# Another order for the delta-rule rounds of a two-layer decoder step

## The chip, the cores and the metric

The kernel runs on one core of a Trainium2 chip. The metric is device time in microseconds (us) of one execution, median of several; lower is better. A core has TensorE (PE, with its weight loads as PEld), VectorE (DVE), ScalarE (ACT), GpSimd (POOL) and SyncE (SP), which in this kernel issues nearly all DMAs. Each engine works off its own list of instructions in order and waits on semaphores for the others.

## The reference, cut to what matters

One inference step of a two-layer trunk, on 512 prompt tokens and 8 x 4 sample tokens: a retention layer, then a gated delta-rule layer, each followed by a mixture of experts. All is float32. The change touches only the delta-rule mixer:

```python
def _gated_delta_chunked(q, k, v, g, beta, s0):
    def step(s, xs):
        ...
        a = jnp.where(strict, jnp.einsum('bhid,bhjd->bhij', kb, ki) * decay, 0.0)
        sol = lax.linalg.triangular_solve(eye + a, rhs, left_side=True, lower=True, unit_diagonal=True)
        u = sol[..., :DN_DV] - sol[..., DN_DV:] @ s
        att = jnp.einsum('bhid,bhjd->bhij', qi, ki) * decay
        o = (qi * jnp.exp(G)[..., None]) @ s + att @ u
        s = (s * jnp.exp(g_last)[..., None]
             + jnp.einsum('bhjd,bhjv->bhdv', ki * jnp.exp(g_last - G)[..., None], u))
        return s, o

def _deltanet_mixer(h, s0, buf, w_in, ...):
    p = h @ w_in
    qkv, buf_new = _causal_conv(p[..., :DN_CONV_CH], buf, conv_w)   # 4 taps, 4096 channels
    qkv = jax.nn.silu(qkv).astype(F32)
    ...
    o, s = _gated_delta_chunked(q, k, v, g, beta, s0.astype(F32))
    o = _rms_norm(o, norm_g) * jax.nn.silu(z...)
    return o.reshape(B, L, DN_VW).astype(h.dtype) @ w_out, ...
```

There are 16 value heads. The prompt has a state that starts at zero; each of the 8 sample sequences brings its own states and gets them back updated.

## The kernel before

The function `delta` (from L1010) computes this mixer. The 16 heads go in four **groups** of four heads; the 512 prompt tokens go in four **chunks** of 128. Chunk `i` of group `g` has the number `x = 4 g + i`, and two chunks share one run `p` of the triangular solve.

The input product is cut into 78 **units** (the list `UNITS`), each of eight matmuls (the items `("mm", U, k)`, k from 0 to 7). Units of features have 512 columns in the first ten and 272 columns afterwards (two halves for one 128-channel column); units of the gate z have 512 columns; a unit of sample rows issues 64 small matmuls, all at k = 7. Units 10 + 21 g to 30 + 21 g belong to the time in which group g is worked on and bring the features of the next group.

One list, the generator `schedule`, sets the order on all engines at once. Each engine walks through it and does its part of every item, in that order. The steps of a group are:

- **A1, AD, A3, A5** (each chunk): transposed keys, decays, scalars, attention and solve matrices.
- **L0, X, P, X5, P5, X6, P6** (each run of the solve): levels of a block inversion. PE multiplies, DVE masks, subtracts and transposes; for P5, X6 and P6 ACT makes copies (L1830, L1838, L1841) on which the next PE step waits.
- **CV, C1, C2, C3, C4, C5** (each chunk, one after another because of the state S): transposed values; products with S; u; the update of S and the output `ob` (DVE L2116, L2127; ACT squares the output, L1818); the norm (DVE L2132, POOL power L1974); in C5 DVE multiplies `ob` by the norm and z (L2140), PE transposes it (L1494), ACT copies it to `oTr` (L1823), SP stores it.
- **SA, SB, SX, SP, S1, S2, S3, SO, SN, SE** (samples of the group). S1 multiplies the sample states with keys and queries (L1596), for head pair 0, then 1; S2 solves. **S3** comes four times a group, for each head pair and each half of the sequences: DVE spreads u over four sequences (`ue`, L2236), PE multiplies (L1617), DVE updates eight states (L2242). After the second half SP stores the states of the pair (L1300) and, when they are out, loads the next pair's into the same tile (L1238).
- **CO** writes rows of the convolution out.

`merge` puts lists together by a place between 0 and 1 for each entry. In groups 0 to 2 the mm items are spread over the first 95% of the group's steps, so that the last C3, C4 and C5 of a group stand without any. In group 3 there are few units left, and eight products of the modulation (AM, four parts each, L221) and four tiles of the first part of the output product (OP, eight matmuls each, L1660) are spread instead.

Around the mm items hang the convolution and its activation. At k = 3 of unit U, DVE convolves unit U-1 if that completes a column: one `tensor_scalar` and three `scalar_tensor_tensor` (L2052, L2054), in one go. At k = 7 ACT applies silu to it (L1777). SP loads the next blocks of weights (2 MB each, L177) at k = 0 of the first unit of a block, through a ring of three slots.

## Time and profile before

| | |
|---|---|
| median of 3 runs | 2101.22 us (2099.69 to 2122.41) |
| profiled execution | 2105.92 us, of which the span of instructions is 2104.1 us |
| mean granted TensorE clock | 0.929 |
| busy: PE, DVE, ACT, POOL | 1820.2, 794.4, 379.0, 357.6 us |
| delta rounds, groups 0 to 3 | from about 1038 to 1747 us of the span |

The profile shows one execution. A row of the timeline gives the start, the duration, engine, line, operation, what is written and read, how many instructions are merged, and in brackets how long the engine stood idle before it and who released it. The clock of PE is given as a share of full speed; 0.5 is the lower of its two levels.

### The profile page before, as it was taken

The numbers are of one execution on the slowest core, as the hardware profiler recorded it, in microseconds if no ns is written. First come the engines' busy times: TensorE is split into PE (matmuls) and PEld (weight loads), VectorE is DVE, ScalarE is ACT, GpSimd is POOL, SyncE is SP. The second block draws the span as 40 slices with busy tenths as digits, with TensorE's granted clock in tenths as the row PEclk, the third lists the DMA queues.
The fourth block names the chain that finished last, engine by engine and source line by source line (L and its number), as shares of the span: only waits on it lengthen the run. The fifth ranks groups of instructions, "written<-read, shape, count | busy, mean of one in ns | idle before, by whom it ended". The sixth has DMA issues, their size and how long they took to land. (4 is left out here: it accounts for less than half of the span.)

```text
span 2104.1 us, 37009 instructions
## 1 busy us (share of the span) xinstructions
PE 1820.2 (87%) x15669; PEld 970.9 (46%) x15669; DVE 794.4 (38%) x1655; ACT 379.0 (18%) x839; POOL 357.6 (17%) x461
## 2 busy tenths in 40 slices
PE   6999999999999678957979989988989888949990
PEld 4344444444434333324556665765665463433320
DVE  0233332323424320034665455546544442450006
ACT  1001000000000011124332242232223110002112
POOL 0020110201103100022421022031113000320006
PEclk9999999999999879987999999999999999969995
DMA  9546657465551299988431034033124548158993
GB/s 327 190 164 232 257 200 256 143 230 200 171 201 50 86 390 401 399 302 266 135 97 48 12 114 126 9 112 92 43 59 170 195 158 270 60 215 320 401 359 137
DMA packets 237630, 399.62 MB, mean 190 GB/s; under 512 B 17993, under 2 KB 94017, under 8 KB 237410
## 3 DMA queue, kind: packets, MB, share of 16 engines
q1 hardware_dynamic: 231514, 375.75, 51.3%
q0 software_dynamic: 5952, 21.50, 2.7%
q8 instruction: 125, 2.05, 0.4%
q14 instruction: 39, 0.32, 0.0%
HBM read 303.71 MB, written 93.51 MB: 189 GB/s over the span
## 5 line engine op out<-in xcount | busy, mean ns | idle before, releaser
L686 PE MATMUL bank<-ring,hT 128*128 128x512 f32 x704 | 319.5, 601 | 1.9 <-DVE ret_qk L904 1.9
L1361 PE MATMUL bank<-hT,ring 128*128 128x272 f32 x768 | 217.0, 417 | 0.0
L686 PEld LDWEIGHTS bank<-ring,hT 128*128 128x128 f32 x704 | 129.6, 191 | 170.0 <-issue 169.8
L2541 PE MATMUL bank<-expert_w,exp_xT 128*32 128x512 f32 x1152 | 178.1, 626 | 15.3 <-DMA expert_w<-in_moe_w_gu_dram 11.4
L1361 PEld LDWEIGHTS bank<-hT,ring 128*128 128x128 f32 x768 | 140.7, 197 | 33.6 <-issue 8.9
L1355 PE MATMUL bank<-ring,hT 128*128 128x512 f32 x256 | 124.8, 616 | 0.0
L3354 PE MATMUL bank<-ring,oT 128*128 128x512 f32 x248 | 114.3, 622 | 0.8 <-PEq L580 0.8
L2541 PEld LDWEIGHTS bank<-expert_w,exp_xT 128*32 128x32 f32 x1152 | 47.9, 115 | 126.4 <-issue 121.2
L2637 DVE TENSOR_TENSOR exp_a<-bank,exp_sg 128x256 f32<-128x256 f32 x24 | 10.2, 424 | 218.9 <-ACT exp_sg L2619 218.9
L978 DVE SCALAR_TENSOR_TENSOR ret_Ss<-ret_Ss,ret_sdec,bank 128x512 f32<-128x512 f32 x64 | 45.0, 744 | 121.3 <-PE bank L772 121.3
L2054 DVE SCALAR_TENSOR_TENSOR dn_y<-dn_pre,dn_conv,dn_y 128x568 f32<-128x568 f32 x96 | 89.1, 928 | 3.4
L2565 PE MATMUL bank<-expert_w,exp_aT 128*32 128x512 f32 x576 | 87.2, 595 | 1.7 <-ACT exp_aT L2601 1.4
L3354 PEld LDWEIGHTS bank<-ring,oT 128*128 128x128 f32 x248 | 49.0, 199 | 62.0 <-issue 62.0
L1355 PEld LDWEIGHTS bank<-ring,hT 128*128 128x128 f32 x256 | 45.9, 194 | 44.6 <-issue 43.6
L1358 PE MATMUL bank<-hT,ring 128*128 128x512 f32 x128 | 57.8, 602 | 1.4 <-ACT dn_smpT L1764 1.4
L2541 PE MATMUL bank<-oT,exp_xT 128*32 128x512 f32 x384 | 56.5, 594 | 0.0
L493 ACT ACTIVATE hT<-bank 128x512 f32<-128x512 f32 (+1 forms) x26 | 13.4, 569 | 213.9 <-PE bank L483 213.9
L2593 DVE COPY exp_y<-bank 128x512 f32<-128x512 f32 x24 | 16.6, 691 | 89.3 <-PE bank L2565 89.3
L848 POOL TENSOR_TENSOR ret_gate<-ret_gate,ret_gn 128x512 f32<-128x512 f32 x16 | 20.3, 1269 | 176.1 <-ACT ret_gate L814 176.1
L3354 PE MATMUL bank<-end_extra,oT 128*128 128x512 f32 x112 | 49.2, 592 | 0.0
L221 PE MATMUL bank<-ring,cT 128*32 128x128 f32 x1280 | 49.1, 298 | 0.0
L1974 POOL TENSOR_TENSOR dn_rso<-dn_sso,eps 128x4 f32<-128x4 f32 x16 | 16.8, 1047 | 173.9 <-DVE dn_sso L2134 173.9
(531 smaller groups left out, 2719.3 us busy)
## 6 DMA issues: line engine op xcount, KB each, us to landing
expert_w<-in_moe_w_gu_dram SPq DMA_DIRECT2D x24, 2048.0 KB, 16.9
ring<-in_w_ada_dram SPq DMA_DIRECT2D x20, 2048.0 KB, 9.5
expert_outputs<-ret_zeros SPq DMA_DIRECT2D x15, 2048.0 KB, 10.4
expert_w<-in_moe_w_down_dram SPq DMA_DIRECT2D x24, 1024.0 KB, 17.4
ret_Ss<-in_state_ret_dram SPq DMA_DIRECT2D x32, 512.0 KB, 5.2
out_dram<-ret_Ss SPq DMA_DIRECT2D x32, 512.0 KB, 3.3
oT<-in_moe_w_gu_dram SPq DMA_DIRECT2D x8, 2048.0 KB, 20.6
ring<-in_dn_w_in_dram SPq DMA_DIRECT2D x8, 2048.0 KB, 9.2
```

Of the source, the lines that this page charges most:

```text
L221: last = pe.matmul(bank[NS * j:NS * (j + 1), 0:P], self.cT[:, k, :], self.ring[:, self.slot[w], k, P * j:P * (j + 1)], start=(k == 0), sto ...
L686: last = pe.matmul(ps[u % 2][:, :], core.hT[:, k, tok(t)], core.ring[:, core.slot[w], k, :], start=(k == 0), stop=(k == KD - 1))
L848: pool.tensor_tensor(gate[:, t, :], gate[:, t, :], gn[:, :], ALU.mult).then_inc(s["gate_done"], 1)
L978: dve.scalar_tensor_tensor(Ss[:, y % SLOTS, a, :], Ss[:, y % SLOTS, a, :], sdec[:, 1, h:h + 1], ps[2 + a][:, :], ALU.mult, ALU.add).then_i ...
L1355: mm = pe.matmul(ps[U % 2][:, :], core.hT[:, k, tok(c)], core.ring[:, core.slot[w], k, :], start=(k == 0), stop=(k == KD - 1))
L1358: mm = pe.matmul(ps[U % 2][:, :], core.ring[:, core.slot[w], k, c * P:(c + 1) * P], core.hT[:, k, 0:SEQ], start=(k == 0), stop=(k == KD - 1))
L1361: mm = pe.matmul(ps[U % 2][:, 0:HALF], core.ring[:, core.slot[w], k, c * P:(c + 1) * P], core.hT[:, k, half * HALF:(half + 1) * HALF], sta ...
L1974: pool.tensor_tensor(rso[:], sso[:], core.eps[:, 3:4].broadcast_to([P, 4]), ALU.pow).then_inc(s["rso_done"], 1)
L2054: ins = dve.scalar_tensor_tensor(y[:, 0:n], pre[:, F % 2, k:k + n], t.conv[:, ch, k:k + 1], y[:, 0:n], ALU.mult, ALU.add)
L2541: last = pe.matmul(ps[v][G * j:G * (j + 1), :], xT[:, v, k, G * j:G * (j + 1)], wgu[of[j] % SLOTS][:, k, :], start=(k == 0), stop=(k == KD ...
L2565: last = pe.matmul(ps[2 + c][G * j:G * (j + 1), :], aT[:, w % 2, k, G * j:G * (j + 1)], wdn[of[j] % SLOTS][:, k, c * W:(c + 1) * W], start ...
L3354: last = pe.matmul(ps[2 * (t % 2) + c][0:rows(t), :], values(t)[:, k, :], blocks[2 * (k // KD) + c][:, k % KD, :], start=(k == (KD if apar ...
```

## The change

Only the order of the steps of the delta rounds changes, and how they are cut; each instruction and its operands stay.

1. In groups 0 to 2 the first two units of the next group are taken out of the next group's spread. Their first twelve mm items stand ahead of the group's last C5, the other four behind it. In group 3 the last six OP items stand ahead of the last C5.
2. C5 is cut: its DVE part becomes the step OG, where C5 stood; the rest (PE transposes, ACT copy, SP store) is C5, now behind the next chunk's C3.
3. S3 is cut into UE (DVE spreads u), S3 (PE) and SU (DVE updates the states, SP stores and loads), with places of their own.
4. The solve steps get places written out by hand (SOLVE).
5. A convolution is done in two halves: taps 0 and 1 at k = 3, taps 2 and 3 at k = 5.
6. SP waits for the first `op_in` transfer before it issues the second.

```diff
-                out += [("CV", x + i), ("C1", x + i), ("C4", x + i - 1), ("C2", x + i), ("C5", x + i - 1), ("C3", x + i)]
-            return out + [("C4", x + NC - 1), ("C5", x + NC - 1)]
+                out += [("CV", x + i), ("C1", x + i), ("C4", x + i - 1), ("C2", x + i), ("OG", x + i - 1), ("C3", x + i),
+                        ("C5", x + i - 1)]
+            return out + [("C4", x + NC - 1), ("OG", x + NC - 1), ("C5", x + NC - 1)]
 
         def s_state(g, hp):
-            return [("S1", g, hp), ("S2", g, hp), ("S3", g, (hp, 0)), ("S3", g, (hp, 1))]
+            return [("S1", g, hp), ("S2", g, hp)] + [(what, g, (hp, half)) for half in range(2) for what in ("UE", "S3", "SU")]
...
-                         at={2: (0.05, 0.12, 0.2), 3: (0.55, 0.65, 0.72, 0.8, 0.86, 0.92, 0.98)})
+                         at={0: SOLVE, 2: (0.04, 0.09, 0.13, 0.18, 0.181, 0.23, 0.28),
+                             3: (0.55, 0.62, 0.67, 0.71, 0.76, 0.761, 0.81, 0.86, 0.89, 0.94, 0.99)})
             c = c_steps(g)
-            return out + merge(b_steps(2 * g + 1), c[:10]) + c[10:]
+            return out + merge(b_steps(2 * g + 1), c[:11], at={0: SOLVE}) + c[11:]
+        SOLVE = (0.02, 0.11, 0.18, 0.25, 0.31, 0.38, 0.44, 0.51, 0.57, 0.69, 0.79, 0.87, 0.95)
...
+            yield from products(first[1], first[1] + ahead)
+            for g in range(1, G):
+                mm, *body = list(products(first[g] + ahead, first[g + 1])), *group(g - 1)
+                yield from merge(body[:-1], mm, at={1: [SPREAD * (i + 0.5) / len(mm) for i in range(len(mm))]})
+                fill = list(products(first[g + 1], first[g + 1] + ahead))
+                yield from fill[:-4]
+                yield body[-1]
+                yield from fill[-4:]
+            even = lambda a, b, n: [a + (b - a) * (i + 0.5) / n for i in range(n)]
+            mm, body = list(products(first[G] + ahead, first[G + 1])), group(G - 1)
+            end = 1 - 1 / len(body)
+            yield from merge(body, mm, LAST, OUT, at={1: even(0, 0.2, len(mm)), 2: even(0.25, 0.94, len(LAST)),
+                                                      3: even(0.21, 0.5, 2 * KD) + even(0.5, 0.96, KD + 2) + [end] * (KD - 2)})
...
+                            sp.wait_ge(s["op_in"], 16)
                             sp.dma_start(core.hT[:, :, 2 * P:SEQ], oTd[:, 0:KD, 2 * P:SEQ]).then_inc(s["op_in"], 16)
...
-                    if what == "S3" and h[1] == 1:
+                    if what == "SU" and h[1] == 1:
                         n = 2 * x + h[0]
                         sp.wait_ge(s["sss_done"], 4 * (n + 1))
...
-                    if what == "C5":
+                    if what == "OG":
                         dve.wait_ge(s["rso_done"], x + 1)
...
+                    if what == "SU":
+                        hp, half = l
+                        n = 2 * g + hp
                         dve.wait_ge(s["s3_ps"], 2 * n + half + 1)
...
-                follow(lambda U: None, step, convolve)
+                follow(lambda U: None, step, lambda U: convolve(U, (0, 1)), LATE, lambda U: convolve(U, (2, 3)))
```

## Rows read from the trace of the kernel before

**Rows 1.** Windows, one for each group: PE, PEld, DVE, ACT, POOL busy, then clock.

```profile
1038.00:1221.00 183.00, 158.61 (x2002) 112.50 (x2001) 98.47 (x229) 52.20 (x135) 35.71 (x55) 0.94 0.20 59
1221.00:1395.00 174.00, 156.28 (x2006) 109.53 (x2006) 96.29 (x225) 54.04 (x133) 32.47 (x51) 0.95 0.25 77
1395.00:1571.00 176.00, 156.84 (x1998) 110.49 (x1997) 96.92 (x225) 50.53 (x129) 33.16 (x51) 0.95 0.27 81
1571.00:1747.00 176.00, 151.27 (x2329) 90.58 (x2327) 73.80 (x202) 42.98 (x89) 25.77 (x33) 0.91 0.54 178
```

**Rows 2.** Waits of PE over the four groups: total us, times, longest.

```profile
PE bank L1494 <- DVE dn_ob L2140: 34.7, 11, 6.7
PE bank L1617 <- DVE dn_ue L2236: 19.4, 10, 3.9
```

**Rows 3.** Windows at two points where PE's clock is low.

```profile
1170.00:1180.00 10.00, 8.29 (x57) 6.35 (x56) 5.55 (x12) 1.34 (x3) 0.33 (x2) 0.58 0.10 27
1390.00:1400.00 10.00, 5.76 (x43) 4.16 (x44) 3.55 (x5) 1.24 (x3) 4.43 (x6) 0.51 0.30 85
```

**Rows 4.** Timeline around the end of group 1.

```profile
1382.90 1.14 DVE L2140 SCALAR_TENSOR_TENSOR dn_ob<-dn_ob,dn_rso,dn_z 128x128 f32<-128x128 f32 x4 [1.12 <-POOL dn_rso L1974]
...
1386.64 1.12 DVE L2116 SCALAR_TENSOR_TENSOR dn_S<-dn_S,dn_egl,bank 128x128 f32<-128x128 f32 x4 [2.60 <-PE bank L1483]
...
1391.00 2.52 POOL L1981 TENSOR_TENSOR dn_km<-dn_qr,masks 128x512 f32<-128x512 f32 x2
1391.06 3.13 DVE L2140 SCALAR_TENSOR_TENSOR dn_ob<-dn_ob,dn_rso,dn_z 128x128 f32<-128x128 f32 x4 [1.12 <-POOL dn_rso L1974]
...
1394.24 1.12 PE L1494 MATMUL bank<-ident,dn_ob 128*128 128x128 f32 x4 [6.75 <-DVE dn_ob L2140]
```

**Rows 5.** Timeline: unbroken runs of input products, and a unit of sample rows.

```profile
1226.09 4.29 PE L1361 MATMUL bank<-hT,ring 128*128 128x272 f32 x18
...
1379.92 3.60 PE L1355 MATMUL bank<-ring,hT 128*128 128x512 f32 x8
...
1093.91 1.95 PE L1349 MATMUL bank<-ring,hT 128*32 128x128 f32 x64
```

**Rows 6.** Timeline around the first C5 of group 0.

```profile
1167.01 1.76 DVE L2177 TENSOR_TENSOR dn_TTf<-dn_TT,bank 32x256 f32<-32x256 f32 x4 [3.18 <-PE bank L1518]
1168.89 0.69 PE L1525 MATMUL bank<-dn_TTf,dn_A 32*32 32x32 f32 x32 [1.26 <-DVEq L2180]
...
1170.32 0.87 DVE L2187 COPY dn_X<-bank 32x256 f32<-32x256 f32 x2
...
1172.41 1.11 PE L1494 MATMUL bank<-ident,dn_ob 128*128 128x128 f32 x4 [1.72 <-DVE dn_ob L2140]
1172.82 2.50 DVE L2054 SCALAR_TENSOR_TENSOR dn_y<-dn_pre,dn_conv,dn_y 128x568 f32<-128x568 f32 x3
```

**Rows 7.** Timeline of group 0: the first S3 and the second S1.

```profile
1077.37 1.13 PE L1617 MATMUL bank<-dn_ue,dn_kds 32*128 32x512 f32 x4 [2.97 <-DVE dn_ue L2236]
...
1078.55 2.16 DVE L2242 SCALAR_TENSOR_TENSOR dn_SS<-dn_SS,dn_egls,bank 128x128 f32<-128x128 f32 x8 [1.23 <-PE bank L1617]
...
1099.94 3.62 PE L1596 MATMUL bank<-dn_SS,dn_km 128*32 128x128 f32 x64 [4.08 <-issue]
```

**Rows 8.** Timeline of group 1: sample states out and in, weights, and S1.

```profile
1265.13 1.02 SPq L1300 DMA_DIRECT2D out_dram<-dn_SS  x2
1268.45 2.43 SPq L1238 DMA_DIRECT2D dn_SS<-in_state_dn_dram  x2
1275.73 0.37 SPq L177 DMA_DIRECT2D ring<-in_dn_w_in_dram  x1
...
1275.97 1.95 PE L1596 MATMUL bank<-dn_SS,dn_km 128*32 128x128 f32 x64 [0.27 <-issue]
...
ring<-in_dn_w_in_dram SPq DMA_DIRECT2D x1, 2048.0 KB, 9.3
```

**Rows 9.** Timeline: the end of group 3.

```profile
1742.23 1.12 PE L1494 MATMUL bank<-ident,dn_ob 128*128 128x128 f32 x4 [3.90 <-DVE dn_ob L2140]
```

More of the change, by code:

```diff
@@ L1137, in schedule, with products @@
         def schedule():
-            first = [0] + [10 + 21 * g for g in range(G)] + [len(UNITS)]
-            for g in range(G + 1):
-                mm = []
-                for U in range(first[g], first[g + 1]):
+            first, ahead = [0] + [10 + 21 * g for g in range(G)] + [len(UNITS)], 2
+            def products(start, stop):
+                for U in range(start, stop):
                     for k in range(KD):
-                        mm.append(("mm", U, k))
+                        yield "mm", U, k
@@ L1145, in schedule @@
                         if k == 3 and U and samples(U - 1):
-                            mm.append(("ST", *unit(U - 1)[0:2]))
-                if g == 0:
-                    for item in mm:
-                        yield item
-                        yield from GATE.get(item[1:], ()) if item[0] == "mm" else ()
-                elif g < G:
-                    head = 2 * KD if g == 1 else 0
-                    yield from mm[:head]
-                    mm = mm[head:]
-                    yield from merge(group(g - 1), mm, at={1: [SPREAD * (i + 0.5) / len(mm) for i in range(len(mm))]})
-                else:
-                    even = lambda a, b, n: [a + (b - a) * (i + 0.5) / n for i in range(n)]
-                    yield from merge(group(g - 1), mm, LAST, OUT, at={1: even(0, 0.29, len(mm)), 2: even(0.3, 0.96, len(LAST)),
-                                                                      3: even(0.29, 0.5, 2 * KD) + even(0.5, 0.99, 2 * KD)})
+                            yield "ST", *unit(U - 1)[0:2]
@@ new lines, in schedule @@
+            for item in products(0, first[1]):
+                yield item
+                yield from GATE.get(item[1:], ()) if item[0] == "mm" else ()
+            yield from products(first[1], first[1] + ahead)
[6 more added lines that the diff above has]
+                yield from fill[-4:]
@@ L1200, in delta, with follow @@
         quad = lambda q: slice(NS * q, NS * (q + 1))
-        def follow(project, step, later=None, late=LATE):
+        def follow(project, step, later=None, late=LATE, rest=None):
             for item in schedule():
@@ L1209, in follow @@
                         later(item[1] - 1)
+                    if rest and item[2] == late + 2 and item[1] > 0:
+                        rest(item[1] - 1)
                 else:
@@ L2057, in convolve @@
                             chain(ins)
-                    ins.then_inc(s["conv_done"], 1)
+                        else:
+                            ins.then_inc(s["conv_done"], 1)
                 def chunk_step(what, x):
@@ L2227, in sample_step @@
                                                  ).then_inc(s["rs_done"], 1)
-                    if what == "S3":
+                    if what == "UE":
                         hp, half = l
```

15 lines of the change are left out of this document (9 added, 6 removed).

## The prediction

> **What bounds the kernel now.** I looked first for the stretch that the change touches: by its lines the delta rounds run from 1038 to 1747 us. The windows by group say that PE is busy 623 of these 709 us, DVE 365, ACT 200 [rows 1]. So PE is the bound, and what can be won is what it loses: 24 us of idle time in group 0, 18 in group 1, 19 in group 2, 25 in group 3, together 86. The clock column adds a second loss: a mean of 0.94, 0.95, 0.95 and 0.91 means that 11, 9, 9 and 16 us, together some 45, went missing as clock, part of it while PE stood idle anyway. The clock falls where PE has just been idle: 0.51 in the 10 us in which the wait of 6.75 us ends, 0.58 in those behind 1.26 and 1.72 us [rows 3, 4, 6]. 0.5 is 1.2 GHz, 1.0 is 2.4.
>
> The waits of PE name two steps for 54 of the 86 us: the transposes of C5, which wait for DVE's multiplication by norm and z (34.7 us, 11 times), and the product of S3, which waits for DVE's `ue` (19.4 us, 10 times) [rows 2]. The timeline then says why. At the end of a group there is no filler: after the last C3 come DVE's update of S, the output, the square, the reduction, POOL's power and DVE's multiplication, and PE stands for 6.75 us [rows 4]. In the middle of a group DVE works in order, with the convolution and eight state updates ahead of what PE waits for [rows 6, 7]. The rounds are followed by a stage that needs all of them, so time saved here shortens the kernel.
>
> **Part 1: two units around the last transposes.** In unbroken runs a product of 272 columns takes 4.29/18 = 0.24 us, one of 512 columns 3.60/8 = 0.45, a unit of sample rows 1.95 [rows 5]. Twelve of the first kind are 2.9 us. At the end of groups 0 and 1 the wait of 6.7 falls by that, and by some 0.4 for the four transposes of chunk 2, which now also stand there: 3.3 us each. At the end of group 2 the twelve items are the sample unit and four products of 512 columns, 1.95 + 1.8, with the transposes 4.1 us. At the end of group 3 six OP products (2.7) and the transposes take 3.1 of 3.90 [rows 9]. Sum: **13.8 us**. The products leave the next group's spread, which has work enough: 21 units either way. The remaining wait is the chain itself; its last link takes 3.13 us beside POOL's masks instead of 1.14 without them [rows 4], and that stays. Items that move on SP: the two weight loads of the next group's first unit come some us earlier and wait for products that are done, at no cost.
>
> **Part 2: OG and C5 apart.** The other seven waits for L2140 are 34.7 - 6.75 x 3 - 3.90 = 10.6 us, and the X5 in front of the first one waits 1.26 in group 0 [rows 2, 6], say 3 over the groups. These 13.6 go, since OG now stands six to eight products ahead of its transposes. But something else is late there. In the new order of the second solve run, C3 comes ahead of P5 and X6, and P6 ahead of the next CV. ACT works in order: square of C3, copies of P5, silu of the convolution, copy of C5, copy of X6. The square waits for DVE, which has the four last subtractions and three transposes (1.76 + 1.3), OG (1.14), the copies for X5 (0.87), the first convolution half (0.5 + 0.8), and C3's own updates (1.12 + 0.7) in front of it, 8.5 us behind P of level 4 [rows 4, 6]. PE gets through C2, X5, C3, P5, C5 and nine small products in 7.4. With 0.6 for the square and 0.8 for two copies, X6 waits some 2.6 us, and P6 some 1.5 more for the silu and the copy behind it: 4.1 us in groups 0, 1 and 2; in group 3, without convolutions, some 2. Behind that, CV of the last chunk now follows C5 at a distance of two products and waits for ACT's copy, 0.7 us a group, and group 3 has one filler less between C2 and C3 (0.8). Sum of part 2: 13.6 - 14.3 - 3.6 = **-4 us**. It could be +8 if ACT's queue proves shorter than I count, and -10 if the convolution's halves come later than at k = 5.
>
> **Part 3: UE, S3, SU.** Between L0 and the product of the second S3, DVE is the bound in groups 0 to 2: the convolution takes 3.0 us (0.5 and three times 0.83), eight updates 2.16 [rows 6, 7], and L0, two `ue`, X, P, A1 and AD of the same timeline some 7.3, together 12.5 of 14 to 16 us. AD moves behind the second `ue` and PE gets more products ahead of each S3, so I expect some 11.5 to 12. From there to the second S1 a DMA chain decides: the last state update, 1 MB out, 1 MB in. In group 1 before it takes 10.5 us from the store's issue at 1265.13 and ends just as PE comes (0.27); in group 0, with weights right behind it, 13, and PE waits 4.08 [rows 7, 8]. The last updates now come about 1.3 us later (behind X of level 2), but PE has 1.6 to 2.4 us more of work before S1. In group 1 the order on SP turns round: the first item of unit 39, with its load of 2 MB, comes ahead of SU, where before it came behind. These weights take 9.3 us [rows 8]; the state exchange is issued some 2 us behind them. No row shows an exchange behind weights. Its cost lies between nothing and the 9.3 us; I take it that it moves behind them but for those 2 us, since already weights on its heels go with a chain that is 2.5 us longer (group 0): S1 then waits some 7 us instead of 0.27. Put together over L0 to S1, idle time in PE was some 12.6, 5.2 and 5.3 us in groups 0, 1, 2 by adding its gaps in the timeline, and should be 8.5, 6 and 2.5: +6. The S3 steps of the second head pair and of group 3 wait 19.4 less the 10.5 of the first pairs, 8.9; I leave 3 of these: +6. Sum: **+12 us** (0 to 20; 20 if the exchange is not held up, 0 if each later S1 has to wait the full chain).
>
> The Trainium skill, "DMA: Bandwidth & Descriptors", section "Queues, rings and completion order", speaks against this part: a queue such as SP's has one ring on each of the 16 engines, and descriptors are taken in ring order. By that rule the state exchange has no way past the weights and group 1 loses the 7 us; if the transfers shared the engines evenly, it would lose about 4, and the sum would be 3 us better. The trace before has the two in the other order only, so it doesn't decide.
>
> **Parts 4 to 6.** SOLVE places are in the numbers above. The cut of the convolution costs no instruction; each DVE step between the halves makes the silu later, and ACT then stands with the copies behind it. Whether PE feels it is the rival below; here I put 0 on it outside part 2, bounded by +3 (a `ue` no longer stuck behind 3.0 us) and -10. The `op_in` wait comes when that load is long in: 0.
>
> **The sum.** 13.8 - 4 + 12 = 22 us of idle time out of 86. The missing 45 us of clock sit behind idle stretches; if they fall by the same quarter that is 11, of which some 3 were in idle time: +8. Together **30 us**: the profiled execution would fall from 2105.9 to 2076, and the median, 4.7 below the profiled one, from 2101.2 to **2071**.
>
> **The rivals.** About 1% (21 us) is what a measurement of this kernel can tell from no change.
>
> *The waits come back elsewhere.* Only part 1 holds; X6, P6 and S1 take all that C5 and S3 give. For it: DVE is busy 98 us in a group of 174 to 183 and more than that where PE waits [rows 1], and none of its work goes. Against: PE idles 24 and DVE 80 us in a group, so order can help. The time: 13.8 and a little clock, 2085 to 2092.
>
> *The clock comes back almost wholly.* If only the long stalls cost clock, then with the 6.75s cut and the 1.7s gone two thirds of the 45 return: 22 + 25, 2055. For it: 0.58 behind 1.26 and 1.72 us shows how dear small waits are [rows 3, 6]. Against: waits of 3 to 7 us remain at each group's end, at X6 and at S1.
>
> *ACT becomes the bound of the middle (slower).* 24 convolutions stand in groups 0 to 2; each silu waits for the second half, which DVE does behind a step of up to 2.16 us [rows 7], and us, u and the solve's copies are queued behind the silu. If it reaches PE fully, that is 24 x 2.16 = 52 us against 30 gained: 2123. It decides the sign from 30 us on, or 1.25 us per convolution. Against: ACT is busy 54 of 174 us [rows 1], and most convolutions have no copy for PE next behind them.
>
> *The cut does nothing:* the wait for L2140 merely moves with the steps and PE's gaps are as long as before: 2101.
>
> **How the numbers follow.** Chances: forecast, 2060 to 2082, 0.43; waits come back, 0.25; clock comes back, 0.15; ACT the bound, 0.10; nothing, 0.07. Faster by over 1% (under 2080): forecast for the most part and the clock case, 0.57. Within 1%: waits come back, nothing, and the rest of the forecast, 0.33. Slower: 0.10. The range from 2050 to 2098 holds the first three; its low end takes part 3 at +20 with all of the clock, its high end part 2 at -10 with part 3 at 0.
>
> **What the profile after would show.** PE's waits for L2140: from 34.7 to about 15, 3 to 3.5 at the ends of groups 0 to 2 and about 1 in group 3. For L2236: from 19.4 to under 9. A new wait of PE at L1540 or L1547 (X6, P6) for ACT's copies, 2 to 4 us a group; a wait of about 7 us at L1596 in group 1, with SP's weights issued ahead of the store of states. The clock by group 0.95 to 0.97. The prediction is wrong if the idle time returns at lines that I do not name, if ACT waits for L2054 grow by over 1 us a convolution, or if the clock stays at 0.94 though idle time fell.

## The result and the profile after

The changed kernel takes 2051.09 us (median of 4 runs, 2041.15 to 2056.60) against 2104.03 us for the kernel before beside it. The ratio of the repeated runs is 0.9716, with a 95% interval of 0.968 to 0.975; the two medians alone give 0.975, at the end of that interval. A second set of runs of the same kernel, told below, gave 0.9702 (0.9672 to 0.9733). So the change is worth 53 us by the first medians and about 60 us by both ratios, up to twice the 30 us that I forecast. The profiled execution took 2056.6 us with a mean clock of 0.932.

The windows of the kernel after: first the whole of the delta rounds, from the first product of the input to the first of the output, then one for each group as in [rows 1]:

```profile
973.20:1698.30 725.10, 684.76 (x8720) 454.13 (x8721) 402.41 (x925) 221.53 (x546) 167.25 (x218) 0.96 0.37 114
1046.00:1216.00 170.00, 162.75 (x2028) 115.37 (x2027) 100.65 (x229) 53.39 (x138) 39.47 (x55) 0.96 0.24 72
1216.00:1381.00 165.00, 154.72 (x2006) 109.19 (x2006) 95.28 (x225) 51.35 (x132) 35.51 (x51) 0.97 0.28 81
1381.00:1543.00 162.00, 155.68 (x2047) 108.44 (x2046) 95.81 (x225) 50.25 (x128) 34.58 (x50) 0.96 0.27 80
1543.00:1698.30 155.30, 138.80 (x2252) 83.49 (x2251) 72.64 (x202) 40.25 (x86) 27.77 (x34) 0.95 0.61 201
```

The same stretch of the kernel before:

```profile
965.67:1746.89 781.22, 693.86 (x8720) 459.72 (x8721) 404.71 (x925) 225.81 (x550) 157.05 (x218) 0.94 0.34 106
```

The stretch is 56.1 us shorter. PE's idle time is the first number less the second: 781.2 - 693.9 = 87.4 us before, 725.1 - 684.8 = 40.3 after. So 47 us are idle time and 9 are busy time. The instructions are the same and the granted clock of the stretch is 0.96 instead of 0.94, so I put the 9 down to the clock. In the other profiled execution of the changed kernel the stretch took 712.8 us with PE busy 668.1: idle 44.7, clock 26. In this pair idle time differs by 4.4 us and busy time by 16.6, so the experiments below are read by idle time, and a difference in it of 4 us or less says nothing.

The waits of PE after, which answer to [rows 2]:

```profile
PE bank L1528 <- issue: 7.4, 3, 3.5
PE bank L1585 <- DVE dn_TTs L2228: 4.4, 3, 1.9
PE bank L1518 <- issue: 4.4, 4, 2.1
PE bank L1518 <- DVE dn_TT L2172: 4.2, 4, 1.3
PE bank L1627 <- DVE dn_ue L2250: 3.9, 3, 1.8
PE bank L1606 <- issue: 3.7, 1, 3.7
PE bank L1518 <- DVE dn_TT L2183: 3.2, 4, 1.4
PE bank L1504 <- DVE dn_ob L2154: 1.6, 2, 0.8
...
PE bank L1557 <- ACT dn_A L1848: 0.7, 1, 0.7
```

The wait in front of C5's transposes (now L1504, for L2154) fell from 34.7 to 1.6 us, the one for `ue` (L1627, for L2250) from 19.4 to 3.9. New is a wait of 4.4 us at L1585, the solve of the sample rows at the start of groups 0 to 2. It comes mainly with the cut convolution, whose second half now stands at k = 5 ahead of the steps of that solve on DVE: with tails and OG but the convolution whole at k = 3 this wait is 0.7 us, with the tails and the whole convolution at k = 5 it is 7.1, and the changed kernel with its convolution whole again has 1.3. The X steps of the solve (L1518, before L1508) wait more as well, 11.8 us in the three rows above (15.5 in the second profile) where the kernel before had 5.5. X5 no longer waits (3.2 us before). Of the waits for ACT's copies that I forecast at X6 and P6, 0.7 us stands there, once.

The tail of group 0 after, where [rows 4] have one of before:

```profile
1208.39 5.67 PE L1371 MATMUL bank<-hT,ring 128*128 128x272 f32 x24
...
1211.61 2.53 POOL L1991 TENSOR_TENSOR dn_km<-dn_qr,masks 128x512 f32<-128x512 f32 x2
1211.68 3.14 DVE L2154 SCALAR_TENSOR_TENSOR dn_ob<-dn_ob,dn_rso,dn_z 128x128 f32<-128x128 f32 x4 [1.12 <-POOL dn_rso L1984]
...
1214.87 0.66 PE L1504 MATMUL bank<-ident,dn_ob 128*128 128x128 f32 x4 [0.82 <-DVE dn_ob L2154]
```

DVE's product beside POOL's masks still takes 3.14 us and the chain is as long as ever. But the twelve products ahead of C5 are **24** instructions of PE and cover 5.67 us of it. The page of the whole kernel says the same:

```profile
L1371 PE MATMUL bank<-hT,ring 128*128 128x272 f32 x768 | 214.5, 413 | 0.0
```

48 units of 272 columns have 8 products each, 384 together, and the page counts 768 instructions: each float32 product is two. (The 214.5 us are the whole kernel's, stretches at low clock included, and the mean of 413 ns counts overlapping instructions, so neither is the price in an unbroken run.)

The clock in the two places of [rows 3] that answer, beside the first C5 of group 0 and the tail of group 1:

```profile
1170.00:1180.00 10.00, 10.00 (x123) 8.11 (x122) 8.19 (x19) 3.98 (x12) 0.33 (x2) 1.00 0.01 2
1375.00:1385.00 10.00, 9.18 (x71) 7.11 (x71) 4.75 (x9) 2.40 (x8) 3.98 (x5) 1.00 0.96 317
```

PE is busy without a gap in the first and the clock stays at 1.00, where it had been 0.58; in the second it is 1.00 where it had been 0.51.

### The profile page after: what moved, and what is told of

It reads as the page before. It is cut to its first block and busy times, and to the rows that moved or that the text cites. A ratio compares the mean times of both kernels' runs of the same rounds, so it can differ in the third digit from the quotient of the medians.

```text
span 2054.8 us, 37012 instructions
## 1 busy us (share of the span) xinstructions
PE 1816.4 (88%) x15669; PEld 967.1 (47%) x15669; DVE 791.3 (39%) x1655; ACT 374.7 (18%) x835; POOL 368.3 (18%) x461
## 5 line engine op out<-in xcount | busy, mean ns | idle before, releaser
L1371 PE MATMUL bank<-hT,ring 128*128 128x272 f32 x768 | 214.5, 413 | 0.0
L1371 PEld LDWEIGHTS bank<-hT,ring 128*128 128x128 f32 x768 | 139.4, 195 | 36.1 <-issue 11.8
L848 POOL TENSOR_TENSOR ret_gate<-ret_gate,ret_gn 128x512 f32<-128x512 f32 x16 | 20.3, 1269 | 176.1 <-ACT ret_gate L814 176.1
L2610 DVE COPY exp_y<-bank 128x512 f32<-128x512 f32 x24 | 16.6, 691 | 88.9 <-PE bank L2582 88.9
L221 PEld LDWEIGHTS bank<-ring,cT 128*32 128x32 f32 x1280 | 37.4, 120 | 26.0 <-issue 22.4
## 6 DMA issues: line engine op xcount, KB each, us to landing
expert_outputs<-ret_zeros SPq DMA_DIRECT2D x15, 2048.0 KB, 10.5
oT<-in_moe_w_gu_dram SPq DMA_DIRECT2D x8, 2048.0 KB, 20.9
```

Of the source, the lines that this page charges most:

```text
L221: last = pe.matmul(bank[NS * j:NS * (j + 1), 0:P], self.cT[:, k, :], self.ring[:, self.slot[w], k, P * j:P * (j + 1)], start=(k == 0), sto ...
L848: pool.tensor_tensor(gate[:, t, :], gate[:, t, :], gn[:, :], ALU.mult).then_inc(s["gate_done"], 1)
L1371: mm = pe.matmul(ps[U % 2][:, 0:HALF], core.ring[:, core.slot[w], k, c * P:(c + 1) * P], core.hT[:, k, half * HALF:(half + 1) * HALF], sta ...
L2610: eng.tensor_copy(y[:, w % 2, W:D], ps[3][:, :]).then_inc(s["y_kept_dve"], 1)
```

## The experiments

The table has every run. "Rounds" is the stretch of the delta rounds in the profiled execution, "idle" that length less PE's busy time in it; both from one execution, while the ratio to the kernel before is from repeated runs.

| kernel | ratio | 95% interval | rounds, us | idle, us |
|---|---|---|---|---|
| before | 1 | | 781.2 | 87.4 |
| + tails | 0.9976 | 0.9949 to 1.0002 | 770.8 | 81.6 |
| + OG apart from C5 | 0.9943 | 0.9914 to 0.9972 | 768.3 | 74.8 |
| + S3 in three | 0.9990 | 0.9963 to 1.0016 | 779.0 | 85.2 |
| + tails, convolution at k = 5 | 0.9945 | 0.9917 to 0.9973 | 773.3 | 78.4 |
| + tails, OG | 0.9810 | 0.9784 to 0.9836 | 746.1 | 59.6 |
| + tails, OG, S3 | 0.9803 | 0.9764 to 0.9843 | 739.7 | 56.8 |
| after | 0.9716 | 0.9682 to 0.9750 | 725.1 | 40.3 |
| after, again | 0.9702 | 0.9672 to 0.9733 | 712.8 | 44.7 |
| after, no tails | 0.9818 | 0.9777 to 0.9859 | 742.3 | 65.8 |
| after, C5 whole | 0.9860 | 0.9821 to 0.9899 | 756.8 | 66.3 |
| after, S3 whole | 0.9822 | 0.9792 to 0.9852 | 747.1 | 59.8 |
| after, convolution whole | 0.9689 | 0.9662 to 0.9716 | 723.9 | 48.8 |
| after, solve spread evenly | 0.9736 | 0.9711 to 0.9761 | 720.1 | 46.4 |
| after, six items in the tails | 0.9748 | 0.9724 to 0.9771 | 728.2 | 53.3 |
| after, weights behind states | 0.9678 | 0.9657 to 0.9699 | 712.5 | 37.9 |
| after, three edits | 0.9675 | 0.9646 to 0.9705 | 710.4 | 39.5 |

### The tails alone

```diff
 (the kernel before, with the schedule of the change)
+                yield from merge(body[:-1], mm, at={1: [SPREAD * (i + 0.5) / len(mm) for i in range(len(mm))]})
+                fill = list(products(first[g + 1], first[g + 1] + ahead))
+                yield from fill[:-4]
+                yield body[-1]
+                yield from fill[-4:]
...
+                            sp.wait_ge(s["op_in"], 16)
```

The same edit gives the items of group 3 new places, as in the change.

> The kernel before with the changed function that orders the items and nothing else (and the wait on op_in): two next units around each last C5, six OP products in group 3; C5, S3, the convolution and the solve's places stay as they were. Theory A (a product is two instructions of PE, 0.47 us for 272 columns and 0.9 for 512, so twelve of them cover 5.7 us of each tail): PE's waits in the four tails fall from 24.1 to under 2.5 us, the clock gives back some 3 more, and the time is 2076 to 2082. Theory B (the prediction's price, 0.24 us a product): waits of 3.2 to 3.3 us stay in three tails, 2087 to 2092. Theory C (most of the gain is clock that comes back once the long waits are gone): below 2070.

Measured: 0.9976, that is 3 to 5 us, and 2104.92 against 2108.22; the interval reaches to 1.0002, so this is hardly told from nothing. All three theories missed the time. The tails did what theory A said: by the timeline the last C5 waits 1.26 and 1.25 us in groups 0 and 1 and nothing over 0.5 in groups 2 and 3. But the wait for DVE's product as a whole fell only from 34.7 to 30.7 us:

```profile
PE bank L1499 <- DVE dn_ob L2145: 30.7, 12, 4.8
PE bank L1622 <- DVE dn_ue L2241: 19.6, 14, 3.0
```

The tails gave 21.6 us and the other C5s took 17.6 of them. Half of that, 9.0 us, stands at the first C5 of groups 0 to 2. The timeline of this kernel at the first C5 of group 0:

```profile
1170.49 0.52 DVE L2057 TENSOR_SCALAR dn_y<-dn_pre,dn_conv 128x568 f32<-128x568 f32 x1
1171.05 2.50 DVE L2059 SCALAR_TENSOR_TENSOR dn_y<-dn_pre,dn_conv,dn_y 128x568 f32<-128x568 f32 x3
1173.46 1.14 DVE L2145 SCALAR_TENSOR_TENSOR dn_ob<-dn_ob,dn_rso,dn_z 128x128 f32<-128x128 f32 x4
...
1174.65 1.12 PE L1499 MATMUL bank<-ident,dn_ob 128*128 128x128 f32 x4 [4.68 <-DVE dn_ob L2145]
```

In [rows 6] the product by norm and z stands **ahead** of the convolution and PE waits 1.72 us. Here the convolution, 0.52 + 2.50 us, stands ahead of it, and PE waits 4.68. Nothing at C5 was edited; the 19 units that are left in the spread of a group fall on other places than 21 did, and the convolution hangs on its unit's k = 3. It happens at the first C5 of groups 0, 1 and 2 (4.68, 4.80, 4.68, where it was 1.72 three times).

The other 8.6 us have no convolution in front. The C5 of the third chunk waits 1.55 us in each of these groups where it did not wait over 0.5 before: between the update of S and C5 the order now has one input product where it had three. The C5 of the second chunk waits 1.78 in group 1, and the first three of group 3, which has no convolutions, wait 7.6 instead of 4.9. There the filler is shorter; no run tests it singly.

### OG apart from C5 alone, and S3 in three alone

```diff
-                out += [("CV", x + i), ("C1", x + i), ("C4", x + i - 1), ("C2", x + i), ("C5", x + i - 1), ("C3", x + i)]
+                out += [("CV", x + i), ("C1", x + i), ("C4", x + i - 1), ("C2", x + i), ("OG", x + i - 1), ("C3", x + i),
+                        ("C5", x + i - 1)]
...
-                    if what == "C5":
+                    if what == "OG":
```

> The kernel before with C5 cut into OG and C5 and nothing else. Theory A (the cut takes the waits of the middle, 10.6 us and the 1.3 in front of the first X5, and makes none): 8 to 14 us under the kernel before; the tails keep their 24 us. Theory B (the prediction's part 2: new waits at X6 and P6 for ACT's copies, and at CV): 2 to 8 us over the kernel before, with waits of 2 to 4 us a group for ACT.

Measured: 0.9943, 12 us (6 to 18): theory A. PE waits at C5 in the four tails only, and no wait for ACT of over 0.8 us is there.

```profile
PE bank L1495 <- DVE dn_ob L2141: 21.7, 4, 6.4
PE bank L1618 <- DVE dn_ue L2237: 20.4, 10, 5.3
```

The other one:

```diff
-            return [("S1", g, hp), ("S2", g, hp), ("S3", g, (hp, 0)), ("S3", g, (hp, 1))]
+            return [("S1", g, hp), ("S2", g, hp)] + [(what, g, (hp, half)) for half in range(2) for what in ("UE", "S3", "SU")]
...
+                         at={2: (0.04, 0.09, 0.13, 0.18, 0.181, 0.23, 0.28),
+                             3: (0.55, 0.62, 0.67, 0.71, 0.76, 0.761, 0.81, 0.86, 0.89, 0.94, 0.99)})
```

> The kernel before with S3 cut into UE, S3 and SU at their new places, and nothing else. Theory A (this part needs no other: its waits for ue, 19.4 us in the kernel before, go by itself): PE waits under 6 us for ue, 15 to 25 us under the kernel before, 2085 to 2095. Theory B (like the first part it pays only beside the others, since an order of steps that suits one spread of products collides with a convolution in another): under 8 us of gain, with waits for ue or for a level of the solve of over 10 us.

Measured: 0.9990, nothing (at most 8 us): theory B. The waits of PE show how the gain is spent:

```profile
PE bank L1499 <- DVE dn_ob L2149: 43.1, 12, 6.7
PE bank L1601 <- DMA dn_SS<-in_state_dn_dram: 12.1, 2, 7.0
...
PE bank L1622 <- DVE dn_ue L2245: 2.1, 1, 2.1
```

The wait for `ue` fell by 17 us, from 19.4 to 2.1. But C5 has the convolution ahead of its product again (4.80, 4.68 and 4.68 us at the first C5 of groups 0 to 2, in all 43.1 instead of 34.7), and S1 of the second head pair waits 7.0 and 5.1 us for the states in groups 1 and 2, and 3.1 in group 0, because PE now gets there before they land: 15.2 us in all where it was 7.0. So half of what `ue` gives goes to C5 and half to S1.

### The convolution moved, with the tails

```diff
-                follow(lambda U: None, step, convolve)
+                follow(lambda U: None, step, convolve, LATE + 2)
```

> The kernel before with the two units around the last transposes (as in the run of that part alone), and in addition every convolution at k = 5 of its unit instead of k = 3, still in one go. In the run of that part alone PE waited 4.68, 4.80 and 4.68 us for the product by norm and z at the first C5 of groups 0 to 2, with a convolution of 0.52 + 2.50 us right ahead of that product on DVE; in the kernel before the product came first, the convolution behind it, and the wait was 1.72. Theory A (taking two units out of the spread shifted the products against the steps, and so the convolution in front of C5's product): the three waits fall back to 1.7 to 2.0 us, together 9 us less, and the time is 5 to 12 us under that run, 2092 to 2100. Theory B (the waits come from fewer products between the steps): they stay over 4 us and the time within 4 us of that run.

Measured: 0.9945, and three waits of 1.72, 4.68 and 1.72 us. In groups 0 and 2 the convolution at k = 5 falls behind the product and the wait is that of [rows 6] to the hundredth; in group 1 it still falls ahead of it, and there the wait stays. So at the first C5 it is the order on DVE and not a lack of filler: theory A for the cause, in two groups of three. All waits at C5 fell from 30.7 to 23.4 us; the 1.55 of each third chunk and those of group 3 stay to the hundredth, so they are not the convolution's. It took some of the gain elsewhere: 7.1 us in front of the samples' solve, 21.8 for `ue` instead of 19.6. The ratio is 3 thousandths lower, with intervals that overlap.

### Parts together

Tails and OG, in the kernel before (both edits above):

> The kernel before with two parts of the change: two units around the last transposes, and C5 cut into OG and C5. S3, the convolution and the solve's places stay as they were. Alone, the first part left the time where it was, since the waits for DVE's product by norm and z that went from the tails (24.1 to 2.5 us) came back in the rows of the middle (10.6 to 28 us). Theory A (the filler that goes to the tail is missed in the middle only by that one step, and a C5 behind the next C3 no longer needs it): both sets of waits go, 30 to 38 us under the kernel before, 2070 to 2080. Theory B (the missing filler makes other steps wait, such as X6, P6 and CV, as the prediction had it): 0 to 12 us under the kernel before, with waits for ACT's copies.

Measured: 0.9810, 40 us: theory A. Singly the two are worth 5 and 12. The waits of PE in this kernel:

```profile
PE bank L1623 <- DVE dn_ue L2242: 23.0, 10, 4.1
PE bank L1524 <- issue: 6.2, 6, 2.4
```

No wait for `ob` stands among the longer ones; by the timeline only the two of 0.82 and 0.81 us at the tails are left. Between DVE's product and the transposes the order now has C3 each time, and beside it eight input products, X5 and P5 at the first C5 of groups 0 to 2, four or three at the second, and one or none at the third. That is less than the "six to eight products" of the prediction at most places, and it is enough.

All three step orders, but the solve evenly spread and the convolution in one go:

```diff
 (the kernel after)
-                         at={0: SOLVE, 2: (0.04, 0.09, 0.13, 0.18, 0.181, 0.23, 0.28),
+                         at={2: (0.04, 0.09, 0.13, 0.18, 0.181, 0.23, 0.28),
...
-            return out + merge(b_steps(2 * g + 1), c[:11], at={0: SOLVE}) + c[11:]
+            return out + merge(b_steps(2 * g + 1), c[:11]) + c[11:]
...
-                follow(lambda U: None, step, lambda U: convolve(U, (0, 1)), LATE, lambda U: convolve(U, (2, 3)))
+                follow(lambda U: None, step, lambda U: convolve(U, (0, 1, 2, 3)))
```

> The three parts that move steps and nothing else: two units around the last transposes, OG apart from C5, S3 cut in three; the solve's steps spread evenly and the convolution in one go, as before. Theory A (these three are the change): a ratio within 0.004 of the changed kernel's 0.970 to 0.972, 2048 to 2060 us. Theory B (written places and halves each replace the other when one of them is gone, and are missed when both are): 2065 us or more, with waits at X6 of over 1 us a group.

Measured: 0.9803, 2071.04 us: theory B. Below, each of the two is missed little or not at all when the other stays. Against those two runs idle time is 8 to 10 us more, of which 5 stand at X6 (7.9 us against 2.5 and 2.8), and PE is busy 8 to 9 us longer at a granted clock of 0.96 instead of 0.97. The timeline at the X6 of group 0:

```profile
1178.15 2.50 DVE L2067 SCALAR_TENSOR_TENSOR dn_y<-dn_pre,dn_conv,dn_y 128x568 f32<-128x568 f32 x3
...
1181.73 0.68 DVE L2141 TENSOR_TENSOR dn_ob<-dn_ob,bank 128x512 f32<-128x512 f32 x1
1182.44 0.63 ACT L1828 ACTIVATE dn_sqo<-dn_ob 128x512 f32<-128x512 f32 x1 [9.10 <-DVE dn_ob L2141]
1182.98 0.36 ACT L1840 ACTIVATE dn_TTf<-bank 32x256 f32<-32x256 f32 x1
1183.36 0.37 ACT L1842 ACTIVATE dn_TTf<-bank 32x256 f32<-32x256 f32 x1
...
1183.78 1.97 PE L1550 MATMUL bank<-dn_TTf,dn_A 64*64 64x64 f32 x16 [2.49 <-ACT dn_TTf L1842]
```

This is the chain that the prediction's part 2 worked out for the changed kernel: the convolution, S, the output, ACT's square in order ahead of the copies, X6. That the wait is 2.49, 2.53 and 2.50 us where 2.6 was forecast is luck. Here ACT's second copy is done 11.6 us behind P of level 4 and PE has 9.1 us of work in between; the forecast had 9.9 and 7.4.

### Parts taken out of the changed kernel

No units around the last C5 (the old order of items):

> The kernel after with the old function that orders the items: nothing stands around the last C5 of a group, all else of the change stays. Theory A: waits of 6.7, 6.7, 6.7 and 3.9 us come back at the tails, with some clock: 25 to 29 us over the kernel after, 2076 to 2080. Theory B (prediction's price): 14 us, 2065 to 2070. Theory C: over 2085.

Measured: 0.9818, 2073.02 us, 21 to 24 us over the kernel after by the ratios. The waits at the tails are 6.30, 6.31, 6.31 and 3.46 us, theory A; the time lies between the forecasts of A and B.

C5 in one piece at its old place:

```diff
-                out += [("CV", x + i), ("C1", x + i), ("C4", x + i - 1), ("C2", x + i), ("OG", x + i - 1), ("C3", x + i),
-                        ("C5", x + i - 1)]
+                out += [("CV", x + i), ("C1", x + i), ("C4", x + i - 1), ("C2", x + i), ("C5", x + i - 1), ("C3", x + i)]
...
-            return out + merge(b_steps(2 * g + 1), c[:11], at={0: SOLVE}) + c[11:]
+            return out + merge(b_steps(2 * g + 1), c[:10], at={0: SOLVE}) + c[10:]
...
-                    if what == "OG":
+                    if what == "C5":
```

> The kernel after with C5 in one piece at its old place, ahead of the next chunk's C3; all else of the change stays. Theory A (the cut of C5 takes away 13.6 us of waits and makes none, since PE has twice the work in front of X6 and P6 that the prediction counted): PE waits some 10 to 13 us for DVE's multiplication again, 2062 to 2067. Theory B (the prediction's part 2: new waits of X6 and P6 cost more than is gained): 2045 to 2049, so faster than the kernel after. A third view, that the other pieces of the change moved C5 out of the way already: within 3 us of the kernel after.

Measured: 0.9860, 2084.64 us, 30 to 33 us over the kernel after: dearer than any theory had it. PE waits 28.8 us in 11 places for the product.

S3 in one piece at its old places:

```diff
-            return [("S1", g, hp), ("S2", g, hp)] + [(what, g, (hp, half)) for half in range(2) for what in ("UE", "S3", "SU")]
+            return [("S1", g, hp), ("S2", g, hp), ("S3", g, (hp, 0)), ("S3", g, (hp, 1))]
```

> The kernel after with S3 in one piece (spread of u, product, update) at its old places; C5, the tails and the convolution in halves stay as in the change. Theory A (the cut takes 15.5 us of waits for ue, and costs 3.7 us before S1 in group 1, since the state exchange then comes behind weights): waits for ue back at 15 to 19 us, the S1 wait of group 1 gone, 2061 to 2066. Theory B (the halves of the convolution have shortened DVE's queue, and that took the waits for ue away): waits for ue under 8 us, within 5 us of the kernel after.

Measured: 0.9822, 2073.74 us, 22 to 25 us over the kernel after. The wait for `ue` is back at 20.3 us, and that of S1 in group 1 is gone: theory A for the mechanism, at a somewhat higher price.

The convolution in one go:

```diff
-                follow(lambda U: None, step, lambda U: convolve(U, (0, 1)), LATE, lambda U: convolve(U, (2, 3)))
+                follow(lambda U: None, step, lambda U: convolve(U, (0, 1, 2, 3)))
```

> The kernel after with the convolution in one go again (four taps at k = 3); all else of the change stays. The earlier runs leave this part open: the three parts undone singly cost 22, 36 and 25 us against the kernel after, more than its whole gain of 60, so they carry each other. Theory A (what PE waits for are steps that now have room of their own, so a DVE queue of 3.0 instead of 1.7 us in one piece costs little): 0 to 6 us over the kernel after. Theory B (the halves matter, because a wait for ue, for a level of the solve or for OG's product comes back behind each whole convolution): 12 us or more over it, with waits for DVE of 1 to 2 us in several places of each group.

Measured: 0.9689, not to be told from the kernel after: theory A. X6 waits 0.68, 1.14 and 0.69 us, P6 1.6 in all, and the X steps (L1518) 20.9 instead of 11.8 and 15.5 in the two profiles of the kernel after; but the samples' solve waits only 1.3 instead of 4.4, and `ue` is not among the longer waits.

The solve spread evenly:

```diff
-                         at={0: SOLVE, 2: (0.04, 0.09, 0.13, 0.18, 0.181, 0.23, 0.28),
+                         at={2: (0.04, 0.09, 0.13, 0.18, 0.181, 0.23, 0.28),
...
-            return out + merge(b_steps(2 * g + 1), c[:11], at={0: SOLVE}) + c[11:]
+            return out + merge(b_steps(2 * g + 1), c[:11]) + c[11:]
```

> The kernel after with the solve's steps spread evenly, as before, in place of the places written out. Theory A: the places are a small matter; 0 to 6 us over the kernel after, with other waits of PE for the solve's masks and transposes (L0, X, P), some longer, some shorter. Theory B: the order of C3, X5, P5, X6 and OG in the second run is what makes the cut of C5 pay; evenly spread, PE waits at X5 or X6 for 1 to 3 us a group and the time is 10 us or more over the kernel after.

Measured: 0.9736, 2 to 3 thousandths over the kernel after with intervals that overlap. X6 waits 0.81, 0.85 and 0.82 us; S1 waits 12.9 us in the four groups, against 3.7 and 7.3 in the two profiles of the kernel after. So written places alone (0.7 to 1.1 left) and halves alone (0.8 left) each take most of the 2.5 us at X6; without both the ratio is 0.980.

### The price of one product

```diff
-                yield from fill[:-4]
+                yield from fill[:-10]
                 yield body[-1]
-                yield from fill[-4:]
+                yield from fill[-10:]
```

> The kernel after with six items ahead of the last C5 of groups 0 to 2 instead of twelve, and ten behind it. Theory A (a product of 272 columns is 0.47 us of PE): the waits of 0.82 us in groups 0 and 1 become 3.6 (0.82 + 6 x 0.47), in group 2, where the six are sample rows and wide products, 3 to 5; together some 9 us more idle time and 2057 to 2063. Theory B (0.24 us a product): 2.3 us in groups 0 and 1, and 2053 to 2056.

Measured: the three last C5 of groups 0 to 2 in the timeline of PE:

```profile
1203.23 0.66 PE L1504 MATMUL bank<-ident,dn_ob 128*128 128x128 f32 x4 [3.56 <-DVE dn_ob L2154]
...
1370.80 0.66 PE L1504 MATMUL bank<-ident,dn_ob 128*128 128x128 f32 x4 [3.55 <-DVE dn_ob L2154]
...
1531.52 1.09 PE L1504 MATMUL bank<-ident,dn_ob 128*128 128x128 f32 x4 [4.48 <-issue]
```

Six products fewer make the wait 3.56 - 0.82 = 2.74 us longer, 0.46 us each, which settles it for theory A. The time, 2056.12, lies at the border of both forecasts: idle time is 9 to 13 us more, the ratio 0.9748 against 0.9702 and 0.9716.

### The weights behind the states

```diff
-                        if item[2] == 0 and item[1] in first and item[1] > 0:
+                        if item[2] == (item[1] == 39) and item[1] in first and item[1] > 0:
```

> The kernel after, but in group 1 the load of 2 MB of weights for unit 39 is issued one product later, so that it stands behind the exchange of the sample states and not ahead of it; all else stays. Theory A (the exchange of 1 MB out and 1 MB in queues behind weights on SP's queue; 16.2 us from store to S1 against 10.5 in the kernel before, where no weights stood ahead): the chain falls back to 10 to 12 us, the wait of 3.67 us before S1 in group 1 falls under 0.5, the time by 2 to 4 us. Theory B (the transfers share the engines, and the chain is long for another reason, such as the later update of the states): the wait stays over 2.5 us.

Measured: SP and S1 of group 1 in the kernel after, and then with the edit; [rows 8] have the kernel before:

```profile
1255.71 0.41 SPq L177 DMA_DIRECT2D ring<-in_dn_w_in_dram  x1
1257.58 3.73 SPq L1310 DMA_DIRECT2D out_dram<-dn_SS  x2
1266.23 2.31 SPq L1247 DMA_DIRECT2D dn_SS<-in_state_dn_dram  x2
...
1273.78 3.64 PE L1606 MATMUL bank<-dn_SS,dn_km 128*32 128x128 f32 x64 [3.67 <-issue]
```

```profile
1244.43 1.03 SPq L1310 DMA_DIRECT2D out_dram<-dn_SS  x2
1247.80 2.67 SPq L1247 DMA_DIRECT2D dn_SS<-in_state_dn_dram  x2
1250.51 0.79 SPq L177 DMA_DIRECT2D ring<-in_dn_w_in_dram  x1
...
1254.96 1.95 PE L1606 MATMUL bank<-dn_SS,dn_km 128*32 128x128 f32 x64 [0.89 <-issue]
```

From the store's issue to S1 it is 16.2 us with the weights ahead and 10.5 with them behind. S1 waits 3.67 us in the one, 5.72 in the second profile of the same kernel, 0.89 in the other. The issue of the two stores itself takes 3.73 us behind the weights and 1.03 without.

The landings say which of the two theories holds. The weights issued at 1255.71 in the kernel after land 9.1 us later, and the stores, 512 KB each, 9.4 us after their issue in the median, against 4.3 with the weights behind:

```profile
ring<-in_dn_w_in_dram SPq DMA_DIRECT2D x1, 2048.0 KB, 9.1
out_dram<-dn_SS SPq DMA_DIRECT2D x2, 512.0 KB, 9.4
```

So the weights land at 1264.8, no slower than in the kernel before, where the exchange comes ahead of them (9.3 in [rows 8]), and the first store at 1266.2, where SP issues the load that waits for it. In the second profile the weights take 9.8 us and the stores 9.9, and the first store again lands 1.5 us behind the weights. Had the transfers shared the engines evenly, I would expect slower weights and the small stores ahead of them. Theory A for the chain, though 0.89 us of the wait stay where under 0.5 was expected. The ratio is 0.9678, 2 to 4 thousandths under that of the kernel after, with intervals that overlap.

Last, three edits at once (the weights, `fill[:-2]` and `fill[-2:]` for fourteen items ahead of C5, the convolution in one go), and beside it the changed kernel itself:

> The kernel after with three edits that the runs point to: the weights of unit 39 behind the state exchange, fourteen items ahead of the last C5 instead of twelve, and the convolution in one go. Theory A (waits add up: 2.8 to 3.7 us before S1 of group 1, 0.82 twice at the tails, nothing or a few us for the convolution): 2038 to 2044, 8 to 12 us under the changed kernel. Theory B (the parts carry each other, and what one edit gains another takes back): 2046 to 2052.

> The changed kernel itself, unedited, as the measure for the runs beside it: every theory expects 2048 to 2054 us and a ratio of 0.970 to 0.974. Its profiled execution tells how much of the 725.1 us of the rounds in the first profile was clock: the runs that stood closest to it had PE busy 674 to 677 us in the rounds, the first profile 684.8; I expect 716 to 726.

Measured: 2043.55 us, 0.9675, against 2049.62 us, 0.9702. Idle time is 39.5 us against 44.7. The edited kernel is ahead by 5 to 6 us in medians, but the intervals overlap, and the weights alone do as well; whether the tails' last 0.8 us and the whole convolution add anything stays open.

## Why the prediction was wrong in size

The direction, the place and the two named waits were right. The time was not: 2071 forecast, 2051 measured, at the edge of the range. Step by step:

By the ratio the miss is larger than the bare median shows: 0.9716 of the 2101.2 that I started from is 2041.5, below the range of 2050 to 2098.

**Part 1, the price of a product, failed.** "In unbroken runs a product of 272 columns takes 4.29/18 = 0.24 us" divides by the instructions of the row, and a product is two of them. The unbroken runs of [rows 5] are 9 products of 0.48 us and 4 of 0.90. The timeline after has 24 instructions and 5.67 us for twelve products, and the run with six of them prices one at 0.46. So the waits at the tails fell from 24.1 to 1.6 us instead of to 10.3: 22.5 won for 13.8 forecast. The count could be had before: eight products a unit against the x of any row. The "64 small matmuls" of a unit of sample rows, named above, are the same slip: the program issues 32, and the trace has 64 instructions; their price, 1.95 us for the unit, was right.

**Part 2 failed through the same number.** I had the chain of DVE and ACT right (ACT's second copy is done 9.9 us behind P of level 4, as forecast) but let PE get through its nine small products at half their length, so X6 seemed to come early: -4 us forecast. The number of products was off as well: in the timeline 12 or 13 stand there in groups 0 to 2, and PE takes 10.4 to 10.9 us for the stretch where I had 7.4. Nine at the right price would have left X6 a wait of some 0.4 us. In the changed kernel X6 does not wait, nor does CV, and all 10.6 us in the middle, with the X5 waits behind them, are gone. The chain itself is real: with whole convolutions and even places X6 waits 2.5 us for it, though both the chain and PE's work are longer there than I had worked out.

**Part 1's "The products leave the next group's spread, which has work enough" failed too,** and it is the greater lesson. Work was enough, places were not: the shift put a convolution of 3.0 us ahead of C5's product in three groups (9.0 us) and left other C5s less filler (8.6 us), and the tails alone gained 3 to 5 us, not 22. A like shift, there from the longer list of steps, took half of the 17 us of S3's cut when it stood alone, and S1's wait for the states the other half. That also means that the sum over parts was no sum. Singly they give 0.24, 0.57 and 0.10%, together 1.97; taking one out of the whole costs 1.0 to 1.6%. What couples them at the first C5 is DVE's order: a gain at one place moves a convolution of 3 us in front of another, and the loss goes once each step that PE needs has work of PE between it and its consumer. How much of the rest is coupled in this way the runs do not say.

**Part 3 was right in kind and too small.** The wait for `ue` fell by 15.5 us. S1 waited 4.08, 0.27 and 2.65 us in groups 0, 1 and 3 before, 3.67 us once after (1.56 and 5.72 in the second profile). So the part gave 15 to 19 us for 12 forecast. Against that stand waits that I had not named: some 4 us more at the samples' solve, which come mainly with part 5, and 6 to 10 more at the X steps of the solve, which no run puts down to one part. S1 of group 1 waits 3.67 and 5.72 where I had 7: the order on SP was read rightly, but PE comes later than I thought, for the reason of part 1. The exchange takes 16.2 and, in the second profile, 17.0 us behind the weights against 10.5 ahead of them, so it is held up by 5.7 to 6.5. (In the kernel before it takes 1275.97 - 1265.13 = 10.8 us, not the 10.5 of the prediction.) As an estimate, all that is left of the weights' 9.3 us is 7.4, and even sharing would cost the 4 that I gave.

By the Trainium skill ("DMA: Bandwidth & Descriptors", "Queues, rings and completion order") each DMA engine takes the descriptors of a ring in ring order. The landings agree: the stores land 1.4 us and more behind the weights, and the weights are no slower for them. The cost is 1 to 2 us below the 7.4, and no run shows why.

**Parts 4 to 6 at nothing** failed as a pair: each of the written places and the halves is missed little or not at all alone, but without both the kernel is 0.9803, some 20 us slower.

**The clock,** +8 forecast, gave 9 in one profile and 26 in the other. It cannot be told better from these: two executions of one kernel differ by 17 us of busy time in the rounds.

What I expected of the clock by group, 0.95 to 0.97, is what it was.

Of the rivals, "the waits come back elsewhere" is what the single parts do (0.998 to 0.999), but not the change as a whole; "the clock comes back almost wholly" named 2055 for a reason that holds only in part, since 43 to 47 of the 60 us are idle time; ACT did not become the bound (0.7 us of waits for it), and the cut did not do nothing.

## What to carry to other kernels

Price a filler from a row whose count you have checked against the program: products of the source divided by records of the row. When one list orders all engines, a long DVE step in the wrong place is as dear as a missing filler, and moving steps moves it: so either keep several products between every short producer and its consumer, or read the timeline after each part for what now stands ahead. And try such parts together before dropping one that gains nothing alone.

## What the runs showed that I had not expected

A float32 product of 128 x 272 is two instructions of PE of 0.24 us each, in both unbroken runs shown; the transposes of C5, four in the program, are x4 in the rows, one instruction each. The issue of two stores of 0.5 MB takes 3.73 us on SP when 2 MB of weights were issued 2 us before, and 1.03 us when none were; in three more profiles with the weights ahead it takes 3.44 to 4.14. So a load ahead holds up the engine that issues, not only the transfer. That a full queue is the reason is my guess. Two profiled executions of the same kernel had PE busy 684.8 and 668.1 us in the same stretch, with clocks of 0.96 and 0.98. That is 17 us, more than several of the parts under study are worth, so single profiles were compared by idle time.
